# Residual tiles one by one through PSUM, and input square sums on TensorE, in a two-layer encoder kernel

## The reference, cut to what matters

```python
def reference(x, ...):                       # x: (1, 512, 1024) float32, DEPTH = 2
    for l in range(DEPTH):
        h = rms_norm(x, ln_pre_mix[l])
        m = hybrid_mixer(h, w_in[l], ...)    # four attention branches, gated, then @ w_out
        x = x + rms_norm(m, ln_post_mix[l])
        h = rms_norm(x, ln_pre_ffn[l])
        gu = h @ ffn_w_gu[l]
        f = (jax.nn.silu(gu[..., :D_FF]) * gu[..., D_FF:]) @ ffn_w_down[l]
        x = x + rms_norm(f, ln_post_ffn[l])
    return x

def rms_norm(x, g):
    y = x * rsqrt(mean(x * x, axis=-1, keepdims=True) + EPS)
    return y * g
```

## Time and profile before

| | us |
|---|---|
| runs, without a profile | 1916.97, 1914.41, 1917.4 |
| median | 1916.97 |
| the profiled execution | 1920.8 |
| its span, first to last instruction | 1918.7 |

### The profile page before, as it was taken

How to read it: one execution, slowest core, us unless ns; L and a number is a source line. 1 busy time by engine, 2 the same in 40 slices (tenths; PEclk the granted TensorE clock), 3 DMA queues, 4 the chain that set the end, 5 groups by cost and what they waited for, 6 DMA issues and landing times.

```text
span 1918.7 us, 25281 instructions
## 1 busy us (share of the span) xinstructions
PE 1769.5 (92%) x8162; PEld 1423.5 (74%) x8162; DVE 942.5 (49%) x1645; ACT 412.6 (22%) x876; POOL 1132.9 (59%) x1172
## 2 busy tenths in 40 slices
PE   7899999969978999999879999999698799999996
PEld 6678777856667888888667787778566678888885
DVE  4754666585637333310266546566856464333102
ACT  3341313213222111100123413131132211111000
POOL 5536454443366878877574373636335668878774
PEclk9999999989998999999889999999899899999998
DMA  5113122110121222222231141111111213222231
GB/s 213 66 44 97 59 71 84 61 72 23 67 87 45 87 99 98 81 91 104 76 119 66 45 110 67 66 67 67 66 45 44 88 45 109 87 104 79 91 104 61
DMA packets 25775, 151.16 MB, mean 79 GB/s; under 512 B 2955, under 2 KB 4235, under 8 KB 11824
## 3 DMA queue, kind: packets, MB, share of 16 engines
q1 hardware_dynamic: 22176, 141.21, 20.8%
q10 hardware_dynamic: 3504, 8.78, 1.7%
HBM read 147.88 MB, written 4.70 MB: 80 GB/s over the span
## 4 chain that ended last, share of the span: by engine, by line
PE 41%; DVE 5%; issue 3%; POOL 1%; ACT 0%; DVEq 0%; ACTq 0%; POOLq 0%
PE main L610 7%; PE main L506 5%; PE main L508 5%; PE main L507 5%; PE work L506 5%; PE work L507 4%; PE work L508 4%; PE turn L675 1%; PE pv L506 1%; PE pv L507 1%; PE pv L508 1%; DVE c_sq L1256 0%; DVE tiny L1178 0%; POOL x L481 0%; DVE sum_f L1194 0%
## 5 line engine op out<-in xcount | busy, mean ns | idle before, releaser
L448 POOL TENSOR_SCALAR w_hi<-raw 128x512 fp32r<-128x512 f32 (+3 forms) x576 | 394.5, 694 | 728.6 <-PE main L610 416.2
L452 POOL TENSOR_TENSOR w_lo<-raw,w_hi 128x512 fp32r<-128x512 f32 (+3 forms) x576 | 737.0, 1290 | 0.0
L610 PE MATMUL main<-h_hi,w_hi 128*128 128x512 f32 x512 | 213.8, 418 | 25.8 <-DVE gates L1169 25.8
L610 PE MATMUL main<-h_lo,w_hi 128*128 128x512 f32 x512 | 208.0, 406 | 0.0
L610 PE MATMUL main<-h_hi,w_lo 128*128 128x512 f32 x512 | 207.6, 405 | 0.0
L506 PE MATMUL main<-h_hi,w_hi 128*128 128x512 f32 x480 | 192.2, 400 | 16.2 <-DVE h_lo L1150 14.9
L507 PE MATMUL main<-h_lo,w_hi 128*128 128x512 f32 x480 | 189.7, 395 | 0.0
L508 PE MATMUL main<-h_hi,w_lo 128*128 128x512 f32 x480 | 189.7, 395 | 0.0
L506 PE MATMUL work<-h_hi,w_hi 128*128 128x512 f32 x480 | 188.7, 393 | 0.0
L507 PE MATMUL work<-h_lo,w_hi 128*128 128x512 f32 x480 | 188.2, 392 | 0.0
L508 PE MATMUL work<-h_hi,w_lo 128*128 128x512 f32 x480 | 188.0, 392 | 0.0
(11 more groups left out here) (196 smaller groups left out, 3037.1 us busy)
## 6 DMA issues: line engine op xcount, KB each, us to landing
raw<-stream SPq DMA_DIRECT2D x106, 1024.0 KB, 4.8
raw<-stream SPq DMA_DIRECT2D x32, 704.0 KB, 4.0
raw<-stream SPq DMA_DIRECT2D x4, 832.0 KB, 5.1
x<-x_in ACTq DMA_DIRECT2D x4, 512.0 KB, 10.6
t_line<-t_first ACTq DMA_DIRECT2D x2, 1024.0 KB
rpb<-rpb_line ACTq DMA_DIRECT2D x16, 128.0 KB, 6.9
out<-x SPq DMA_DIRECT2D x8, 256.0 KB, 2.2
bias_b<-t_line ACTq DMA_DIRECT2D x2, 768.0 KB, 4.8
```

What stands on the lines that cost most here:

```text
L448: pool.tensor_scalar(w_hi[:, slot, parts[q]], raw[:, slot, parts[q]], 1.0, 0.0, ALU.mult, ALU.add).then_inc(piece_hi, 1)
L452: e = pool.tensor_tensor(w_lo[:, slot, part], raw[:, slot, part], w_hi[:, slot, part].bitcast(F32), ALU.subtract)
L610: mm = pe.matmul(main[m % 2][:, :], w, (h_lo if which == 1 else h_hi)[:, k, :], start=(s % STEPS == 0), stop=(s % STEPS == STEPS - 1))
```

## The change

At each residual that is followed by a norm, every tile now goes alone and in order. VectorE forms the product with the factor in a PSUM bank and adds x to it in that bank, in two banks by turns (`work[2]` and `pv` after the mixer, `main` after the feed-forward part). ScalarE copies the bank to x, waits for its own copy, and makes `h_hi` and the square from x; VectorE makes `h_lo` from the bank. GpSimd has no part in it. The last output of the program keeps its old form.

The eight squares of an input norm are no longer added on VectorE. TensorE multiplies each with the column of 1/1024 and accumulates in PSUM (`square_step`): in the first layer all eight behind the latent projection, in the second after each step of it, at the feed-forward input after each step of piece 0. There the spread moves to a place behind four steps of piece 1's gate half. All hardware loops are written out, in all five programs.

```diff
+        x_bank = [work[2], pv]
...
-                for d in range(MIX_DVE, KD):
-                    pool.wait_ge(scaled, at(l, 2 * KD, d + 1))
-                    pool.tensor_tensor(x[:, d, :], x[:, d, :], kept_m[:, d, :], ALU.add).then_inc(x_pool, 1)
...
+            def square_step(l, name, k):
+
+                t = TURN_AT[("stat", name)]
+                if k == 0:
+                    wait_turn(l, t)
+                pe.wait_ge(squared, at(l, 4 * KD, KD * NORMS.index(name) + k + 1))
+                for tt in range(NT):
+                    mm = pe.matmul(turn[t % 2][:, tt:tt + 1], norm_f["sq"][:, k, P * tt:P * tt + P], mean,
+                                   start=k == 0 and tt == 0, stop=k == KD - 1, skip_group_check=True)
+                if k == KD - 1:
+                    mm.then_inc(turn_done, 1)
...
-                pe.wait_ge(loaded, 16)
-                mean_square(l, "pre_mix")
+                    if l:
+                        square_step(l, "pre_mix", k)
+                if l == 0:
+                    pe.wait_ge(loaded, 16)
+                    for k in range(KD):
+                        square_step(l, "pre_mix", k)
...
-                gate_up(0, 0, (0, 1), first=True)
+                for k in range(KD):
+                    gate_up(0, 0, (0, 1), range(k, k + 1), first=True)
+                    square_step(l, "pre_ffn", k)
                 wait_piece(l, GU0 + 1)
-
-                gate_up(0, 1, (0,), range(2))
-                mean_square(l, "pre_ffn")
-                gate_up(0, 1, (0,), range(2, KD))
-                gate_up(0, 1, (1,), range(1))
+                gate_up(0, 1, (0,), range(4))
                 spread(l, "pre_ffn")
-                gate_up(0, 1, (1,), range(1, KD))
-                with pe.Fori(1, KF // 2) as i:
+                gate_up(0, 1, (0,), range(4, KD))
+                gate_up(0, 1, (1,))
+                for i in range(1, KF // 2):
...
+            def next_input(l, name, done, banks):
 
                 for d in range(KD):
...
+                    act.wait_ge(x_done, done + d + 1)
+                    act.activation(x[:, d, :], banks[d % 2][:, :], ACT.Copy).then_inc(x_kept, 1)
+                    act.wait_ge(x_kept, done + d + 1)
+                    norm_input(l, name, d, x[:, d, :])
...
+            def residual(l, name, then, banks):
...
+                for d in range(KD):
+                    if d >= 2:
+                        dve.wait_ge(x_kept, first + d - 1)
+                        dve.wait_ge(lo_done, at(then, N_SPLIT, SPLIT_AT[("h", to, d - 2)] + 1))
+                    dve.tensor_tensor(banks[d % 2][:, :], kept[:, d, :], factor(l, name), ALU.mult).then_inc(scaled, 1)
+                    dve.wait_ge(scaled, first + d + 1)
+                    dve.tensor_tensor(banks[d % 2][:, :], x[:, d, :], banks[d % 2][:, :], ALU.add).then_inc(x_done, 1)
+                    if d == 0:
+                        dve.wait_ge(params_in_place, 16 * then + 16)
+                    else:
+                        low(d - 1)
+                low(KD - 1)
```

More of the change, by code:

```diff
@@ L406, in load @@
                 sp.dma_start(raw[:, slot, 0:size], src).then_inc(piece_in[slot], 16)
-            with sp.Fori(0, L) as l:
+            for l in range(0, L):
                 for n in range(4):
@@ L472, in free_after @@
                 return main_done, at(l, N_MAIN, MAIN_AT[("y", name[6], KD - 1)] + 2)
-            with pool.Fori(0, L) as l:
+            for l in range(0, L):
                 split(l, 0, 0, PIECES[0][1], (main_done, at(l, N_MAIN, 1)))
@@ L719, in branch_out @@
                     mm.then_inc(main_done, 1)
-            with pe.Fori(0, L) as l:
+            for l in range(0, L):
                 for t in range(3):
@@ L822, in _ @@
                 branch_out(l, "C")
-                with pe.Fori(0, 2) as i:
+                for i in range(0, 2):
                     for s in range(2):
@@ L876, in _ @@
                         gate_up(i, s, (1,))
-                with pe.Fori(0, KD // 2) as i:
+                for i in range(0, KD // 2):
                     for d in range(2):
@@ L995, in _ @@
             act.dma_start(t5_first, t5_row[:, :]).then_inc(t5_sem, 16)
-            with act.Fori(0, L) as l:
+            for l in range(0, L):
                 line = rpb_in[bass.ds(l, 1), :]
@@ L1111, in _ @@
                 keep(l, "post_mix")
-                ffn_input(l)
-                with act.Fori(0, KF // 2) as i:
+                next_input(l, "pre_ffn", at(l, 2 * KD, 0), x_bank)
+                for i in range(0, KF // 2):
                     for s in range(2):
@@ L1232, in wait_work_done, with last_output @@
+            def last_output(l):
+                first = at(l, 2 * KD, KD)
+                for i, d in enumerate([*range(LAST_DVE, KD), *range(LAST_DVE)]):
+                    dve.tensor_tensor(kept_h[:, d, :], kept_h[:, d, :], factor(l, "post_ffn"), ALU.mult).then_inc(scaled, 1)
+                    if d < LAST_DVE:
+                        dve.wait_ge(scaled, first + i + 1)
+                        dve.tensor_tensor(x[:, d, :], x[:, d, :], kept_h[:, d, :], ALU.add).then_inc(x_done, 1)
             def wait_work_done(l, name):
@@ L1346, in gate_outputs @@
                     merged_lo(d)
-            with dve.Fori(0, L) as l:
-                dve.wait_ge(params_in_place, 16 * l + 16)
-                mixer_input(l)
+            for l in range(0, L):
+                steps[0] = 0
+                if l == 0:
+                    dve.wait_ge(params_in_place, 16)
+                    first_input()
+                else:
+                    residual(l - 1, "post_ffn", l, main)
+                    token_factor(l, "pre_mix", r_token)
                 dve.wait_ge(loaded, 16)
@@ L1463, in _ @@
                 output_factor(l, "post_mix")
[L1464 to L1470 removed]
+                residual(l, "post_mix", l, x_bank)
                 token_factor(l, "pre_ffn")
@@ L1474, in _ @@
                 dve.sem_inc(waited, 1)
-                with dve.Fori(0, KF // 2) as i:
+                for i in range(0, KF // 2):
                     for s in range(2):
```

118 lines of the change are left out of this document (45 added, 73 removed).

## The result

The changed kernel takes **1935.45 us** (median of 4 runs, 1934.65 to 1935.84); the kernel before took 1915.69 in the same comparison (4 runs, 1914.34 to 1917.4). The ratio is 1.0102, 95% interval 1.0085 to 1.012: slower by 1.0%, as forecast, at a time within 1 us of the 1936 predicted. Not every step of the sum held, though, and the experiments lead to a version that beats both kernels by more than this change lost.

The account below looks back on a forecast made before the run. TensorE's work plus its holes was taken to bound the kernel; +5.5 (start), -5 (boundary), +20 (feed-forward inputs) and -2 (loops) gave +18.5 us, forecast 1936 us, with 1922 to 1959 to hold 8 times in 10.

Parts of the forecast that it names:

- the sum: Whole program: +5.5 start, -5 boundary, +20 feed-forward inputs, -2 loops, together +18.5 us.
- What bounds the kernel: Whole kernel: time is TensorE's work, busy 92% of the span, plus the holes in it.
- Tiles in PSUM: Residuals before a norm: VectorE needs 2.1 us a tile, first h_lo ready 3.7 us after the first product.
- the list of signs: Profile changes expected after, among them the boundary's wait for h_lo falling from 15.5 us to about 6.
- The boundary, -5 us: Between the layers: first product to first gate matmul 31.0 to 32 us against 36.5, -5 us (-3 to -6.5).
- Squares on TensorE: Input norms: each group of short matmuls costs 0.9 us at full clock, 1.85 at half; eight groups replace one.
- the first rival: Feed-forward inputs: half clock for all eight tiles, +19.5 us each, 1955 us in all; chance 0.38.
- Feed-forward inputs, +10 us each: Both layers, first product to third feed-forward piece: 46.8 us against 36.8, full clock after about half the tiles.
- the sign named for it: Feed-forward input: granted clock stands at 0.50 in the second and third tile.
- The root's price: Feed-forward inputs: root 6.4 us beside GpSimd's splitting, 0.4 for semaphores, leaving a TensorE hole of 2 to 4 us.
- The start, +5.5 us: Start of the program: seven more groups, 5.7 us, and 0 to 4 for the clock, less a shorter root wait; +5.5 us.
- Loops, -2 us: Written-out hardware loops, whole program: -2 us (0 to -4).

Follow-up runs that it names:

- loops_only: The kernel before with its fourteen hardware loops written out and nothing else changed; 1914.46 us, ratio 1.0003.
- pool_after_root: The changed kernel with GpSimd held until the root is done, at the boundary and before each third feed-forward piece; 1919.88 us, ratio 1.0021.
- all_roots_clear: pool_sums_wait with GpSimd also held for the roots of each layer's first token factor and the boundary's output factor; 1893.05 us, ratio 0.9884.
- pool_sums_wait: Changed kernel with start and boundary squares summed on VectorE, feed-forward input squares on GpSimd, which then waits for the root; 1901.52 us, ratio 0.9926.
- squares_only: The kernel before with loops written out and input squares accumulated on TensorE, old residuals kept; 1942.99 us, ratio 1.0148.
- groups_last: The changed kernel with all eight groups of short matmuls behind the feed-forward input's whole first piece; 1932.92 us, ratio 1.01.
- pool_sums: pool_sums_wait without GpSimd's wait for the root before the third feed-forward piece; 1908.74 us, ratio 0.9956.

## Why the prediction was right, and where it was not

**What bounds the kernel.** The reading held: TensorE's work and holes made the time, and the stages that moved most are those named (B and E, the mixers, by -1.5 and +1.0). The cause of the loss was named rightly (groups on TensorE, half clock, the root beside GpSimd's splitting); the size of its parts was not.

**Tiles in PSUM.** Predicted 2.1 us a tile on VectorE and h_lo 3.7 us after the first product; measured 2.17 and 3.6 to its end (1531.99 to 1535.59), TensorE starting after 3.75. The wait at the boundary fell by 11.7 us to 3.84, as the sum had it; the list of signs had "about 6", which does not fit that sum and did not come. Product to first gate matmul is 31.3 us (964.34 to 995.60), inside the 31.0 to 32 forecast. But of the 5.2 us against before, 2.5 belong to the loops: the same distance is 33.9 us in loops_only (950.33 to 984.25).

**The boundary, -5 us: the step that failed is what stands in front of the product.** Measured -2.1, and against loops_only, without the loop's pause, +0.2. I had written that, with the additions gone, GpSimd's splitting starts some 7 us before TensorE wants it, and counted it only as being ready. It starts at 955.16, beside the root of the output factor (956.82 to 962.1), which takes 5.3 us for 2.1 before: +3.1 us. pool_after_root and all_roots_clear show this by taking it away (first statistics matmul to product 6.4 us for 9.5).

**Squares on TensorE, 0.9 us a group at full clock, 1.85 at half.** Measured 0.81 (1545.15 to 1545.96) and 1.56 (1538.43 to 1539.99) alone; with what they cost the matmul behind them, as the prediction counts, 2.27 - 6 x 0.227 = 0.91 and 4.25 - 6 x 0.427 = 1.69. The Trainium skill, page "TensorE: Matmul & The Clock Gate", section "A second HAM failure mode: psum-queue depth-cycling", says that frequent short idling between groups makes the clock swing between its levels. In the changed kernel TensorE has no such pauses between 1543 and 1557, so it is no trial of that rule: full clock was held over six tiles with a group in each, and was lost only in the hole before the spread. With that the first rival, half clock through the whole stage, fell. The trace of pool_sums_wait speaks against the rule here: four pauses of 0.40 to 0.52 us between 1520 and 1527, and a granted clock of 1.00 throughout.

**Feed-forward inputs, +10 us each.** Measured +7.7 and +7.8. By the steps: first product to last group's end 25.3 us (predicted 28.5), from there to the spread 7.6 (6.8), the spread 1.7 (1.3), the 36 matmuls 10.0 (10.2). The mis-sized term is the first: the clock rose after two tiles, not four, worth 2 x (4.25 - 2.27) = 4 us; the sign named for it, 0.50 in the second and third tile, held for the second alone. The hole was 4.59 us where 2 to 4 were forecast. pool_after_root gives the weights: of the 44.7 us, 7.4 are the root's meeting with GpSimd and what the hole does to the clock. My sum had 4.9 for it (6.8 for 3.9, and 2 for half clock).

**The root's price** was taken from the longest wait of the page and put down to the place "where GpSimd splits a piece all the time". That was right, and it was read too narrowly: I priced the collision where the stage had it and did not ask where else the change would bring about the same (the boundary), or what it already cost (the start). The Trainium skill, page "SBUF — State Buffer", section "SBUF: two separate sides", says that a VectorE instruction with two SBUF inputs and a GpSimd instruction lock each other out of a shared pair of ports for a whole instruction. The trace agrees (though line 1177, with one SBUF operand, took 0.40 us for 0.17 as well): the slow steps of the root end where a GpSimd instruction ends (1559.35 and 1559.33, 1561.17 and 1561.16), 1.19 to 1.22 us beside a w_lo (1.24 to 1.29 us) and 0.54 to 0.55 beside a w_hi (0.62), and the residual's products and sums, one of whose operands lies in PSUM, keep 0.69 to 0.70 us beside the same splitting (964.34 on, GpSimd busy to 968.4).

**The start, +5.5 us.** The first gate matmul came at 42.60, as forecast (43), in part by luck: the statistics began at 33.24 for 35.58 and took 9.4 us, of which the forecast had 6.5 and up to 4 for the clock. At the first upward matmul only 1.9 of the 6.2 us are left (59.73 for 57.80; 3.9 against loops_only, whose first matmul stands as early as after's), and 0.4 at the end of the mixers. The step that failed is that the delay was carried through to the end, without asking what is late next: the chain of root, scaling and rotation on VectorE was late already. It started 6.5 us later (51.91 for 45.41), but GpSimd's next splitting, which starts when the gate matmuls are done, 8.8 us later (57.44 for 48.65): 6.2 for the groups and 2.6 for a dozen gate matmuls at half clock. So the rotation stood ahead of the splitting and took 0.63 us for 3.68, and the wait for lat_lo fell from 6.36 us to 1.22:

```profile
56.54 0.63 DVE L1396 TENSOR_TENSOR rope_d<-d_tm,const 128x64 f32<-128x64 f32 x4
```
```profile
59.34 0.63 PE L642 MATMUL turn<-const,d_tm 128*128 128x128 f32 x4 [1.22 <-DVE lat_lo L1153]
```

**Loops, -2 us.** Nothing measurable in the whole time (loops_only). No run shows a cost of register waits at the places where TensorE waits for VectorE. What the traces show instead is VectorE's pause at the loop's turn, worth 2.1 us of TensorE's wait at the boundary. The prediction knew of it inside the 15.5 us and so counted its going in the boundary's -5.

**The sum** was right by errors that cancel. Its terms, costed from the profiled execution of before, came to +18.5 where the spans show +14.6: the feed-forward inputs are 4.5 less, the start 3.6 less, the boundary 2.9 more, and the rest, the loops' -2 with it, 1.3 more. But I added the sum to a median, and that execution turned out 5.1 us longer than the median of before; between the medians the change is +19.8. That execution of before had 6 us more than loops_only's in the stages that I costed (A +2.0, C +0.9, D +2.2, F +0.9). Of this, D goes with the loop's pause, and 1.5 of A with a first latent matmul at 14.70, where the eleven traces without loops have 12.8 to 13.2; C and F differ by when the clock rose and fell. Why the medians of before and loops_only agree all the same is open; only one execution of each was traced. The sign and the ranking of the rivals don't hang on it: C and F alone are +15.5 against one execution and +17.4 against the other.

**What stays open.** The gain from holding GpSimd behind w_out. And when the clock rises among tiles and groups: one tile sooner in pool_after_root than in the changed kernel, in both layers, and in squares_only after four tiles in one layer and one in the other. No run separated what decides it.

## What to carry to other kernels

When an edit frees an engine earlier, look at what that engine will now do sooner and beside whom: at the boundary the additions taken from GpSimd let its splitting slide beside VectorE's chain of eleven tiny steps. Look as well at what the edit moves up to an engine that stays put: at the feed-forward inputs GpSimd splits when piece 0 is done, as before (it idles 27.9 us for it), and the root now falls in just there. Three semaphore waits that hold GpSimd for a few microseconds gave back three quarters of the loss (in the traces about 4 of these 15.6 us are a clock that rose sooner, which the waits don't explain). A serial chain of small VectorE steps on TensorE's path is worth keeping clear of GpSimd wherever it stands; keeping it clear at the feed-forward inputs, the boundary and the start, and giving the feed-forward inputs' sums to the engine that was idle, turned a 1.0% loss into a 1.2% gain. Work moved to the engine that bounds the kernel must fit into its holes; count it at both clock levels, and count the hole that it fills as lost cover.

## What the runs showed of the hardware

VectorE's steps on 128x4 elements take 0.16 us alone and 0.5 to 1.2 us beside GpSimd's work on 128x512, a factor of seven; products on 128x64 took 0.92 us for 0.16. Products and sums of 128x512 with one operand in PSUM were not slowed at all (0.69 to 0.70 us).

A recorded one-column matmul of this type takes TensorE about 0.1 us at full clock (0.81 us for eight) and 0.2 at half, between long ones as in a row. 64 of them in a row at full clock ended with the clock at half in both places where it was looked at (the start of the changed kernel: 1.00 up to 37.8, 0.50 from there; groups_last, from 1548.40: 1.00 up to 1553.4, 0.50 from there).

After a wait of nearly the same length TensorE may stay at half clock for under 4 us or for nearly 20, busy all the while. Behind the wait for the gates (11.9 and 12.1 us) in the second layer's mixers it starts again at 1359.15 in pool_sums and at 1360.12 in pool_sums_wait; the granted clock some microseconds on was, in the one and in the other:

```profile
1363.00:1368.00 5.00, 5.00 (x11) 2.66 (x11) 1.72 (x3) 1.63 (x4) 0.00 (x0) 0.50 0.00 0
...
1377.00:1379.00 2.00, 2.00 (x6) 1.53 (x5) 1.67 (x4) 0.65 (x3) 0.00 (x0) 0.55 0.01 4
```
```profile
1364.00:1369.00 5.00, 4.90 (x18) 2.76 (x17) 2.94 (x6) 2.39 (x6) 0.00 (x0) 1.00 0.01 2
```

It costs 5 to 7 us (E 509.2 for 502.5; B 509.1 in pool_after_root), in a stretch whose instructions are the same. So a difference of this size between two single executions is no measure of an edit elsewhere; the runs of one kernel lie 1 to 10 us apart. Whether the long stretch comes by chance or by the timing that a kernel brings is not shown: one execution of each kernel was traced, and three of the four runs of pool_sums lie within 0.5 us of each other.
